# Frequency-domain products of the long convolutions: complex sums on GpSimd, one inverse product per class

## The reference

```python
def long_conv(z, ks, d):
    zf = jnp.fft.rfft(z, n=2 * L, axis=1)
    return jnp.fft.irfft(zf * ks[None], n=2 * L, axis=1)[:, :L] + d * z

z = x1.astype(F32) * long_conv(v.astype(F32), kspec[:, 0], bias[0])
return x2.astype(F32) * long_conv(z, kspec[:, 1], bias[1])
```

## Time and profile before

| | us |
|---|---|
| median of 3 runs (lowest to highest) | 2406.47 (2402.73 to 2407.73) |
| the profiled execution | 2401.68 |
| its span, first to last instruction | 2399.9 |
| the middle part, from about | 760 to 1157 of the span |

### The profile page before, as it was taken

How to read it: one execution, slowest core, us unless ns; L and a number is a source line. 1 busy time by engine, 2 the same in 40 slices (tenths; PEclk the granted TensorE clock), 3 DMA queues, 4 the chain that set the end, 5 groups by cost and what they waited for, 6 DMA issues and landing times.

```text
span 2399.9 us, 26125 instructions
## 1 busy us (share of the span) xinstructions
PE 2273.4 (95%) x10340; PEld 1859.4 (77%) x10340; DVE 1189.4 (50%) x1655; ACT 786.0 (33%) x1193; POOL 146.3 (6%) x163
## 2 busy tenths in 40 slices
PE   6999999998998989778899999999999999999998
PEld 4778877886786767666688888888888887888886
DVE  6676666654832756656455333343333334324332
ACT  5432333244434434534344211222122122324221
POOL 0221122000111000100000000000000000000000
PEclk9999999999998989999999999999999999999999
DMA  4344444444556665756645111121111112535442
GB/s 144 107 142 133 125 130 138 138 161 138 190 180 175 189 189 154 236 153 185 212 133 175 50 60 53 62 79 53 59 51 62 62 53 89 183 114 174 155 148 85
DMA packets 213588, 307.22 MB, mean 128 GB/s; under 512 B 15481, under 2 KB 143865, under 8 KB 213467
## 3 DMA queue, kind: packets, MB, share of 16 engines
q1 hardware_dynamic: 200858, 256.00, 35.1%
q0 software_dynamic: 11312, 46.14, 5.2%
q10 hardware_dynamic: 1296, 3.41, 0.4%
HBM read 207.38 MB, written 72.16 MB: 116 GB/s over the span
## 4 chain that ended last, share of the span: by engine, by line
PE 51%; DVE 0%; ACT 0%; issue 0%; DVEq 0%; POOL 0%
PE mlp_acc L128 10%; PE mlp_acc L130 10%; PE mlp_acc L129 10%; PE mlp_dacc L128 7%; PE mlp_dacc L130 7%; PE mlp_dacc L129 7%; PE mlp_acc L2597 0%; DVE out_s_lo L2495 0%; DVE up_u L245 0%; ACT up_u L2438 0%; DVE mlp_h_lo L2517 0%; DVE out_w_lo L2490 0%; DVE down_d_lo L2539 0%; ACT out_s_hi L2413 0%; DVE up_u L249 0%
## 5 line engine op out<-in xcount | busy, mean ns | idle before, releaser
L128 PE MATMUL mlp_acc<-mlp_h_hi,up_w_hi 128*128 128x512 f32 x1056 | 411.1, 389 | 0.2 <-DVE mlp_h_lo L2517 0.2
L130 PE MATMUL mlp_acc<-mlp_h_hi,up_w_lo 128*128 128x512 f32 x1056 | 410.8, 389 | 0.0
L129 PE MATMUL mlp_acc<-mlp_h_lo,up_w_hi 128*128 128x512 f32 x1056 | 410.8, 389 | 0.0
L2522 DVE TENSOR_TENSOR up_w_lo<-up_w_raw,up_w_hi 128x1024 fp32r<-128x1024 f32 x44 | 53.8, 1225 | 388.2 <-ACT up_w_hi L2430 388.2
L128 PEld LDWEIGHTS mlp_acc<-mlp_h_hi,up_w_hi 128*128 128x128 f32 x1056 | 198.2, 188 | 41.6 <-DVE mlp_h_lo L2517 0.6
L130 PEld LDWEIGHTS mlp_acc<-mlp_h_hi,up_w_lo 128*128 128x128 f32 x1056 | 198.2, 188 | 41.2
L129 PEld LDWEIGHTS mlp_acc<-mlp_h_lo,up_w_hi 128*128 128x128 f32 x1056 | 198.2, 188 | 41.1
L128 PE MATMUL mlp_dacc<-down_d_hi,down_s_hi 128*128 128x512 f32 x528 | 206.8, 392 | 5.3 <-DVE down_d_lo L2539 5.3
L129 PE MATMUL mlp_dacc<-down_d_lo,down_s_hi 128*128 128x512 f32 x528 | 206.5, 391 | 0.0
L130 PE MATMUL mlp_dacc<-down_d_hi,down_s_lo 128*128 128x512 f32 x528 | 206.4, 391 | 0.0
L2430 ACT ACTIVATE up_w_hi<-up_w_raw 128x1024 fp32r<-128x1024 f32 x44 | 46.6, 1060 | 460.1 <-PE mlp_acc L130 460.1
(11 more groups left out here) (243 smaller groups left out, 3901.4 us busy)
## 6 DMA issues: line engine op xcount, KB each, us to landing
in_w_raw<-arg_w_in_t SPq DMA_DIRECT2D x58, 512.0 KB, 3.6
down_s_raw<-g_scratch SPq DMA_DIRECT2D x48, 512.0 KB, 4.7
up_w_raw<-arg_w_up_t SPq DMA_DIRECT2D x44, 512.0 KB, 3.5
g_scratch<-up_prod POOLq DMA_DIRECT2D x22, 768.0 KB, 3.5
filt_tab<-arg_fwd SPq DMA_DIRECT2D x32, 512.0 KB, 3.8
mix_classes<-mix_split SPq DMA_DIRECT2D x48, 256.0 KB, 7.9
mix_kf<-k_scratch SPq DMA_DIRECT2D x48, 256.0 KB, 3.0
mix_split<-mix_classes SPq DMA_DIRECT2D x48, 256.0 KB, 5.0
```

What stands on the lines that cost most here:

```text
L128: pe.matmul(out, w_hi, x_hi, start=first, stop=False)
L129: pe.matmul(out, w_hi, x_lo, start=False, stop=False)
L130: return pe.matmul(out, w_lo, x_hi, start=False, stop=last)
L2522: dve.tensor_tensor(w_lo[i % 2][:, :, :], raw[i % 2][:, :, :], w_hi[i % 2][:, :, :].bitcast(F32), ALU.subtract).then_inc(sem["w_low"], 1)
```

## The change

- In `multiply` VectorE makes four operations on 64 partitions each, so that both partial products of a real part lie beside each other on partitions 0 to 63 (ac and bd), and both of an imaginary part on 64 to 127 (ad and bc). The fourth has a factor of -1.0 (scalar_tensor_tensor).
- GpSimd adds the two halves of `prod` into a new tile `whole` (128x512, `add_parts`), with a semaphore from VectorE ("crossed") before it and one to TensorE ("multiplied") behind it.
- `inverse` makes one product per class from `whole`. The inner tables have two matrices for each class in place of three, and the sign of the imaginary part has moved into them.
- forward's and `load_after`'s waits are on "crossed", VectorE's wait before it writes `prod` is on GpSimd's sum of two pairs earlier, and GpSimd waits for the inverse of two pairs earlier before it writes `whole`.
- add_mask(j + 1) stands on GpSimd at the first attend step of job j, for jobs 2 to 7.
- The costs in `schedule` are the same as before.

```diff
-            inner[:, t, u, 0] = np.block([[co, -si], [si, co]])[rows]
-            inner[:, t, u, 1] = np.block([[co.T, si.T], [-sign * co.T, -sign * si.T]])[:, rows]
-            inner[:, t, u, 2] = np.block([[-sign * si.T, sign * co.T], [-si.T, co.T]])[:, rows]
+            inner[:, t, u, 0] = np.block([[co, sign * si], [si, -sign * co]])[rows]
+            inner[:, t, u, 1] = np.block([[co.T, si.T], [sign * si.T, -sign * co.T]])[:, rows]
...
+        whole = [p.sb(f"whole{b}", [P, 2, HC]) for b in range(2)]
...
                 def load_after(g):
                     if g + ring < len(pairs):
-                        sp.wait_ge(sem["multiplied"], g + 1)
+                        sp.wait_ge(sem["crossed"], g + 1)
                         load_k(g + ring)
...
+                def add_parts(g):
+                    pr, to = prod[g % 2], whole[g % 2]
+                    if g >= 2:
+                        pool.wait_ge(sem["g_ready"], g - 1)
+                    pool.wait_ge(sem["crossed"], g + 1)
+                    pool.tensor_tensor(to[:, :, :], pr[:, 0, :, :], pr[:, 1, :, :], ALU.add).then_inc(sem["multiplied"], 1)
+
                 for step in schedule:
-                    if step[0] == "load":
-                        add_mask(*step[1:])
+                    if step[0] == "forward":
+                        add_parts(*step[1:])
+                    elif step[0] == "attend" and step[2] == 0 and 1 <= step[1] < len(jobs) - 1:
+                        add_mask(step[1] + 1)
...
                     if g >= 2:
-                        pe.wait_ge(sem["multiplied"], g - 1)
+                        pe.wait_ge(sem["crossed"], g - 1)
...
                     for u in range(2):
-                        for i in range(2):
-                            last = pe.matmul(gacc[:, u, :], tab[s][:, t, u, 1 + i, :], prod[g % 2][:, u, i, :],
-                                             start=i == 0, stop=i == 1)
+                        last = pe.matmul(gacc[:, u, :], tab[s][:, t, u, 1, :], whole[g % 2][:, u, :], start=True, stop=True)
                     last.then_inc(sem["g_ready"], 1)
...
                     if g >= 2:
-                        dve.wait_ge(sem["g_ready"], g - 1)
-                    x, kk = xacc[g % 2], kf[g % ring]
-                    dve.tensor_tensor(prod[g % 2][:, :, 0, :], x[:, :, :], kk[:, :, :], ALU.mult)
-                    dve.tensor_tensor(prod[g % 2][0:SUB, :, 1, :], x[0:SUB, :, :], kk[SUB:P, :, :], ALU.mult)
-                    dve.tensor_tensor(prod[g % 2][SUB:P, :, 1, :], x[SUB:P, :, :], kk[0:SUB, :, :],
-                                      ALU.mult).then_inc(sem["multiplied"], 1)
+                        dve.wait_ge(sem["multiplied"], g - 1)
+                    x, kk, pr = xacc[g % 2], kf[g % ring], prod[g % 2]
+                    dve.tensor_tensor(pr[0:SUB, 0, :, :], x[0:SUB, :, :], kk[0:SUB, :, :], ALU.mult)
+                    dve.tensor_tensor(pr[0:SUB, 1, :, :], x[SUB:P, :, :], kk[SUB:P, :, :], ALU.mult)
+                    dve.tensor_tensor(pr[SUB:P, 0, :, :], x[SUB:P, :, :], kk[0:SUB, :, :], ALU.mult)
+                    dve.scalar_tensor_tensor(pr[SUB:P, 1, :, :], x[0:SUB, :, :], -1.0, kk[SUB:P, :, :], ALU.mult, ALU.mult).then_inc(sem["crossed"], 1)
```

More of the change, by code:

```diff
@@ L344, in split_tables @@
         outer[:, 2 + h] = outer[:, h].T
-    inner = np.zeros((P, len(tiles), 2, 3, P), np.float32)
+    inner = np.zeros((P, len(tiles), 2, 2, P), np.float32)
     m = np.arange(SUB)[:, None]
@@ L404, in __init__ @@
             self.otab = [f.sb(f"otab{s}", [P, 4, P]) for s in range(len(SEQS))]
-            self.tab = [f.sb(f"tab{s}", [P, len(spectral_classes(s)), 2, 3, P]) for s in range(len(SEQS))]
+            self.tab = [f.sb(f"tab{s}", [P, len(spectral_classes(s)), 2, 2, P]) for s in range(len(SEQS))]
             self.cols = [f.sb(x, [P, TT, DIRS, HEADS]) for x in ("a_cols", "floor_cols", "own_cols", "past_cols")]
@@ L416, in __init__ @@
             self.so_raw = [f.sb(f"s_raw{b}", [P, KD, P]) for b in range(2)]
-        self.size = 2 * big * HC + 2 * 4 * P + sum(len(spectral_classes(s)) for s in range(len(SEQS))) * 6 * P + 5 * TT * DIRS * HEADS + DIRS * P + HEADS
+        self.size = 2 * big * HC + 2 * 4 * P + sum(len(spectral_classes(s)) for s in range(len(SEQS))) * 4 * P + 5 * TT * DIRS * HEADS + DIRS * P + HEADS
         self.otab_loaded, self.const_loaded = w.sem("otab_loaded"), w.sem("const_loaded")
@@ L1604, in long_convolutions_and_heads @@
         bank = {x: p.ps(f"bank_{x}", [P, CH]) for x in "abc"}
-        names = ("v_ready v_copied x_ready multiplied g_ready g_copied "
+        names = ("v_ready v_copied x_ready crossed multiplied g_ready g_copied "
                  "y_ready z_ready transposed copied "
```

## The result

The changed kernel takes 2438.73 us, the median of four runs (2432.71 to 2440.64), against 2406.26 us for the kernel before, four runs taken with them (2402.73 to 2407.73). The ratio is 1.0141 with a 95% interval of 1.0127 to 1.0156: slower by 32.5 us, of which I had foretold 22. The profiled execution took 2439.54 us, its span 2437.8.

A forecast was written before the change was run, and what follows sets the result against it. VectorE was taken to set the pace from pair to pair in the middle part; +35.0 -4.4 -6.9 -1.1 +0.6 -1.1 gave +22.1 us, so 2428.5 us from a median of 2406.5, range 2410 to 2446.

The forecast's parts named there:

- the late GpSimd: Rival, dense stretches: hop 1.0 us longer, or sums and norms hold each other up; +17 to 2445 us; chance 0.17.
- term 5: At the starts, pairs 2 and 42, the hop from products through GpSimd's sum to inverse costs +0.6 us beyond the 0.73.
- Term 1: Fourth product on VectorE in each of 48 pairs, 0.73 us each: +35.0 us.
- Terms 2 and 4: Fourth product hidden in six pairs (12 to 15, 18, 28), -4.4 us; a spectrum wait before pair 3 filled, -1.1 us.
- Term 3: Where a turn begins behind an inverse, TensorE leads; the halved inverse saves 0.86 us at eight points: -6.9 us.
- eight points: Behind inverse 11, before pairs 21, 29, 32, 33 and 37, last inverses 39 and 47: TensorE leads, 0.86 us saved each.
- Terms 5 and 6 and the ports: Hop at pairs 2 and 42, +0.6; mask collision before pair 34 gone, -1.1; sums meeting 18 norm operations, 0 to 19, taken nothing.
- a sign of being wrong: On GpSimd: the prediction counts as wrong if the sum takes over 2 us.
- the rule: VectorE with two SBUF inputs and GpSimd reading SBUF lock each other out; all 18 norms held would add 22 us.
- TensorE's lead between links: Rival, between links and attends: 19 pairs gain 0.86 us instead of losing 0.73; -8.1 us, 2398.4 us; chance 0.11.
- the cancelling: Rival: half of 19 link-and-attend pairs gain and TensorE-led turn starts double; total 0, 2401.7 to 2411.3 us; chance 0.11.
- its rule: In some 20 pairs of the dense stretches, what is added to the hop costs half of itself per pair: 10 us.

The follow-up runs named there:

- e1: Kernel before with a fourth VectorE product per pair, its result unused, inverse unchanged, no GpSimd sum: 2437.34 us, ratio 1.0143.
- e2: Kernel before with one product per class in the inverse instead of two, three VectorE products, no sum: 2400.73 us, ratio 0.9989.
- e3: Changed kernel without GpSimd's sum, the inverse reading the first partial product right behind VectorE's products: 2428.94 us, ratio 1.0108 against the kernel before.
- e5: Kernel before with only the masks moved, GpSimd waiting for each pair's products but making no sum: 2401.71 us, ratio 0.9997.
- e4: Changed kernel with each inverse product made twice, the first result overwritten: 2450.33 us, ratio 1.0191 against the kernel before.

## Why the prediction was right, and where it was wrong

The sign, the leading engine and the range were right; the forecast was 10 us short of 32.5. The measured 2438.73 us lies nearer to the late GpSimd's 2445 than to the forecast's 2428.5, and its mechanism had a part in it, as term 5 shows.

**Who leads.** Right: VectorE. e1 costs its whole length, e2 gives at most 5 of 41 us by its runs, and the round between links went from 4.46 to 5.16 us where I had said 5.2.

**Term 1, the fourth product, +35.0.** The duration was 0.684 us and with the step to the next operation 0.70, my lower bound, not 0.73: 33.6 us. The operation with a constant is as fast as a tensor_tensor; the row with a scalar for each partition (0.75) wasn't its neighbour.

**Terms 2 and 4, cover, -4.4 and -1.1.** The cover exists (4.3 us as far as pair 28 in e1, 3.2 of them shorter waits for spectra), but later stretches cost 4.2 us more than the products in them, with the clock lower than before. Net: nothing, where I had taken off 5.5. The sum had no term for such an excess, and that e1 came out at the bare 48 x 0.70 is the chance of two effects of one size.

**Term 3, eight points where TensorE leads, -6.9.** About right with the fourth product in place, -8.4 from e1 to e3. Without it e2 gives 0.2 to 5.3 us by its runs, so the eight points weren't shown one by one.

**Terms 5 and 6 and the ports: -0.5 in the sum, +9.8 measured** for the sum on GpSimd. The moved masks and the collision saved by them are in e3 too, so they aren't in this 9.8; e5 shows 0.6 us for them by the medians, which can't be told from nothing. This is the term that was mis-sized, and the greatest miss. I had both ends, 0 and 19 us, and took nothing, by the argument that the norm operation starts first, so that the sum waits, and that most inverses aren't urgent. The count was right, 19 meetings for 18, and in 11 of them the sum did wait, five times with a length of 2.23 us, which is over the 2 us that I had named as a sign of being wrong. But in 8 the sum was first, and VectorE was held up, 7.6 us over 40 operations, and the inverse waits 9.1 us more for GpSimd than for VectorE in e3. How the 9.8 divides between the two wasn't separated. GpSimd's pickup of 0.15 us and the sum's 1.27 were as estimated; so the length of an undisturbed hop wasn't the miss. The Trainium skill (SBUF — State Buffer, Who interferes with whom) states that such a pair of instructions locks each other out for the whole instruction, and that one with a single SBUF input isn't touched. The rows agree on both: L2082 takes 1720 ns with sums about and 693 without, and the four products of a pair, which read PSUM and one SBUF tile, keep their 679 to 694. The 22 us that the rule gave with all 18 held were three times what VectorE lost.

**Masks, inner tables, spectra.** As foretold: the masks 0.6 us, within the interval, the tables' twelve loads issued from 573.6 to 654.3 us against 572.9 to 652.1, the wait for spectra before L1990 4.6 us where it was 9.0.

**TensorE's busy time.** I foretold 41 us less, and it is 18.9 less in the stretch: it has fewer matmuls and a lower clock. VectorE's is 38.9 more, just over my 34 to 37, by the collisions. I had written no word on the clock.

**The rivals.** TensorE's lead between links falls by e2, and the cancelling by the result itself, 2438.7 us where it had 2411.3 at the most. GpSimd coming late was put as a rival of +17 with a chance of 0.17; its mechanism is at work in the actual result with 9.8 us, and doubling it costs 17.6 where its rule gives 12.

## What to carry to other kernels

Before moving work between engines, ask on which of them the time from one step to the next hangs, by the idle time ahead of its operations: here VectorE had 16.4 us in 48 pairs, and an operation of 0.70 us added there cost 0.70 us for each pair on average, while 0.86 us taken from TensorE was worth 0.1 at most. Near a balance the two directions differ: one product more for each pair costs 34 us in all, one less gives back 16, since the next two limits, loads and matmuls, stand right behind it. A hand-over to GpSimd must be priced with the operations that meet it, on both sides, and not by its own length alone.

## What the runs showed of the hardware

- A GpSimd sum of two SBUF tiles and a VectorE operation with two SBUF inputs delay each other, and it is the second to start that gets longer: 1.27 us became 1.70 or 2.23 for the sum (11 times), 0.69 became 1.72 for L2082 as a mean of four. VectorE operations that read PSUM and one SBUF tile weren't delayed (0.679 to 0.694 us as group means).
- TensorE's granted clock was lower in the dense stretches shown once its work had gaps: 0.91 and 0.85 in place of 1.00, busy for 66% and 67% in place of 89% and 92%. One added VectorE operation for each pair (e1) came with 0.87 in place of 1.00 from pair 36 to 39. Making the inverse's matmuls twice (e4) brought the two dense stretches to 0.97 and 0.90 and left the mean of the whole at 0.92.
- A VectorE scalar_tensor_tensor with a constant and one PSUM input takes 0.684 us on 64x512, the tensor_tensor 0.68 to 0.69.
- GpSimd took up VectorE's signal after 0.15 us. TensorE took up GpSimd's 0.06 us after the end of the sum (869.42 to 869.48).
